# Up projections of the FFN: one 512-column matmul for high and low x in place of two of 256

## What is computed

```python
u = rms_norm_2(h, pre_ffn_norm[i])
up = causal_dwconv(u @ w_up[i], conv_w[i], conv_b[i])     # w_up: 2048 x 11264
gate, val = jnp.split(up, 2, axis=-1)
f = (jax.nn.gelu(gate, approximate=True) * val) @ w_down[i]   # w_down: 5632 x 2048
h = h + rms_norm_2(f, post_ffn_norm[i])
```

## Time and profile before

| | |
|---|---|
| median of 3 runs | 2880.22 us (2879.9 to 2881.02) |
| span of the profiled execution | 2875.0 us |
| instructions | 51385 |
| mean granted TensorE clock over the span | 0.943 of full speed |

### The profile page before, as it was taken

How to read it: one execution, slowest core, us unless ns; L and a number is a source line. 1 busy time by engine, 2 the same in 40 slices (tenths; PEclk the granted TensorE clock), 3 DMA queues, 4 the chain that set the end, 5 groups by cost and what they waited for, 6 DMA issues and landing times.

```text
span 2875.0 us, 51385 instructions
## 1 busy us (share of the span) xinstructions
PE 2619.4 (91%) x22498; PEld 2563.1 (89%) x22498; DVE 1685.9 (59%) x1516; ACT 1104.7 (38%) x1093; POOL 217.8 (8%) x117
## 2 busy tenths in 40 slices
PE   5999999979999787987998999998999999999986
PEld 5999999879999787886886999987999999999986
DVE  4556666475455785284363445557666666666665
ACT  3344545333333351242233333433344444444442
POOL 3000000023400231041000000002000000000000
PEclk9999999989999898798796999998999999999998
DMA  5444444334445342041140555552455555555432
GB/s 189 149 147 157 145 149 144 123 112 155 161 167 180 125 153 80 18 147 44 46 163 29 190 183 182 179 185 109 164 188 184 181 190 177 188 185 180 175 132 88
DMA packets 59615, 419.95 MB, mean 146 GB/s; under 512 B 6464, under 2 KB 8640, under 8 KB 9056
## 3 DMA queue, kind: packets, MB, share of 16 engines
q1 hardware_dynamic: 59280, 417.26, 40.8%
q0 software_dynamic: 208, 0.75, 0.1%
HBM read 415.89 MB, written 2.10 MB: 145 GB/s over the span
## 4 chain that ended last, share of the span: by engine, by line
PE 79%; DVE 13%; ACT 4%; issue 2%; POOL 2%; DMA 0%; SPq 0%; DVEq 0%; ACTq 0%; POOLq 0%
PE banks L206 23%; PE banks L208 23%; PE banks L207 23%; DVE weights_lo_sb L191 3%; ACT weights_hi_sb L185 2%; DVE xa_lo_sb L269 2%; DVE h_sb L259 1%; PE banks L1005 1%; PE banks L240 1%; PE banks L916 1%; PE banks L995 1%; PE banks L1004 1%; POOL rw_tile_sb L1156 1%; PE banks L1389 1%; PE banks L373 1%
## 5 line engine op out<-in xcount | busy, mean ns | idle before, releaser
L206 PE MATMUL banks<-xa_hi_sb,weights_hi_sb 128*128 128x256 f32 (+1 forms) x4800 | 1382.0, 288 | 106.0 <-DVE weights_lo_sb L191 47.2
L191 DVE TENSOR_TENSOR weights_lo_sb<-raw_weights_sb,weights_hi_sb 128x2048 fp32r<-128x2048 f32 x393 | 914.3, 2328 | 800.6 <-ACT weights_hi_sb L185 798.3
L207 PE MATMUL banks<-xa_lo_sb,weights_hi_sb 128*128 128x256 f32 (+1 forms) x4800 | 1376.9, 287 | 0.0
L208 PE MATMUL banks<-xa_hi_sb,weights_lo_sb 128*128 128x256 f32 (+1 forms) x4800 | 1376.7, 287 | 0.0
L185 ACT CAST weights_hi_sb<-raw_weights_sb 128x2048 fp32r<-128x2048 f32 x393 | 748.5, 1905 | 1107.8 <-PE banks L208 1095.4
L206 PEld LDWEIGHTS banks<-xa_hi_sb,weights_hi_sb 128*128 128x128 f32 x4800 | 923.2, 192 | 116.4 <-issue 50.5
L208 PEld LDWEIGHTS banks<-xa_hi_sb,weights_lo_sb 128*128 128x128 f32 x4800 | 923.1, 192 | 0.0
L207 PEld LDWEIGHTS banks<-xa_lo_sb,weights_hi_sb 128*128 128x128 f32 x4800 | 919.5, 192 | 0.5
L206 PE MATMUL banks<-ff_hi_sb,weights_hi_sb 128*128 128x256 f32 x704 | 198.4, 282 | 3.1 <-DVE ff_lo_sb L1887 2.7
L206 PE MATMUL banks<-xb_hi_sb,weights_hi_sb 128*128 128x256 f32 (+1 forms) x688 | 197.2, 287 | 4.0 <-DVE low_flat_sb L1514 1.3
L207 PE MATMUL banks<-ff_lo_sb,weights_hi_sb 128*128 128x256 f32 x704 | 199.7, 284 | 0.0
(11 more groups left out here) (365 smaller groups left out, 2148.0 us busy)
## 6 DMA issues: line engine op xcount, KB each, us to landing
raw_weights_sb<-weights SPq DMA_DIRECT2D x393, 1024.0 KB, 4.8
h_sb<-h SPq DMA_DIRECT2D x1, 2176.0 KB, 8.8
out<-h_sb SPq DMA_DIRECT2D x4, 512.0 KB, 2.8
masks_sb<-consts_rw POOLq DMA_DIRECT2D x1, 352.0 KB, 3.9
params_sb<-params SPq DMA_DIRECT2D x1, 305.5 KB, 8.2
consts_first_sb<-consts_first SPq DMA_DIRECT2D x1, 304.0 KB, 9.4
...
```

The lines of the kernel that those rows point to most:

```text
L191: dve.tensor_tensor(c.w_lo[n % SPLIT][:], c.raw[n % RAW][:], c.w_hi[n % SPLIT][:].bitcast(F32), ALU.subtract).then_inc(c.sem("lo_done"), 1)
L206: pe.matmul(out, w_hi[:, k, a], x_hi[:, tile, cols], start=begin, stop=False)
L207: pe.matmul(out, w_hi[:, k, a], x_lo[:, tile, cols], start=False, stop=False)
L208: done = pe.matmul(out, w_lo[:, k, a], x_hi[:, tile, cols], start=False, stop=end)
```

## The change

The high and low parts of x now lie in one tensor, `xa_both` (128 x 2 x 16 x 272), and `xa` is two views of it. The up projections use a new function, `products_both`. Its first matmul reads high and low x together as 512 columns and writes a whole bank, columns 0 to 255 with high weights by high x, 256 to 511 with high weights by low x. Its second adds low weights by high x. The two halves of a bank are summed when they are taken: ACT copies the upper columns of the four banks to `low_half` (the tile `late_acc`), DVE adds the lower columns (`up_summed`) and then multiplies by `rs`. PE waits for `up_summed` where it waited for `up_out_taken`. The down projections and all other stages keep `products`. Besides, several semaphores are merged into counted ones (`lam_steps`, `zeros`, `rw_taken`, `grams`, `grams_taken`, `ple_steps`), with the same waits; these edits are left out below.

```diff
-        self.xa = [self.sb(ctx, f"xa_{x}", [P, KT, ROWS], F32R) for x in ("hi", "lo")]
+        self.xa_both = self.sb(ctx, "xa", [P, 2, KT, ROWS], F32R)
+        self.xa = [self.xa_both[:, x] for x in range(2)]
...
+def products_both(c, pe, n, x, tiles, outs, cols, first, last, i=None, step=0, pause=None):
+
+    pe.wait_ge(c.sem("lo_done"), at(n + 1, i, step))
+    w_hi, w_lo = c.w_hi[n % SPLIT], c.w_lo[n % SPLIT]
+    length = cols.stop - cols.start
+    for j, out in outs:
+        if pause and j == 3:
+            pause()
+        for k, tile in tiles:
+            a = slice(j * P, j * P + P)
+            begin, end = first and k == tiles[0][0], last and k == tiles[-1][0]
+            pe.matmul(out, w_hi[:, k, a], x[:, :, tile, cols], start=begin, stop=False)
+            done = pe.matmul(out[:, length:], w_lo[:, k, a], x[:, 0, tile, cols], start=False, stop=end)
+    done.then_inc(c.sem("slot_used"), 1)
...
-    first_chunk_pe(c, pe, t, n, c.xa, 3, BOTH, 6, 4)
+    for s in range(4):
+        pe.wait_ge(S("x_ready"), 12 + s + 1)
+        products_both(c, pe, n + s, c.xa_both, t4(s), banks(c, 0, 2 * SEQ), BOTH, s == 0, s == 3)
+    sum_squares(c, pe, t["acc"], 7, BOTH, S("squares_ready"), 4, S("stats_done"))
...
-                pe.wait_ge(S("up_out_taken"), i * 2 + 1)
+                pe.wait_ge(S("up_summed"), i * 2 + 1)
...
-                products(c, pe, n + 8 + 4 * x + s, c.xa, t4(s), banks(c, x, SEQ), BOTH, s == 0, s == 3, i, 12)
+                products_both(c, pe, n + 8 + 4 * x + s, c.xa_both, t4(s), banks(c, x, 2 * SEQ), BOTH, s == 0, s == 3, i, 12)
...
+    def low(x, f, i, done):
+
+        act.wait_ge(S("slot_used"), done)
+        act.copy(t["low_half"][:], c.ps[:, 4 * x:4 * x + 4, SEQ:2 * SEQ]).then_inc(S("up_low"), 1)
...
+    low(0, 0, None, n + 4)
     scaled(0, 0, None)
     for m in range(6, 9):
         split_hi(c, act, n + m)
+    act.wait_ge(S("up_summed"), 1)
+    low(1, 0, None, n + 8)
     gelu(0, None)
     scaled(1, 0, None)
...
         for m in range(1, 13):
+            if m in (5, 9):
+                act.wait_ge(S("up_summed"), at(m // 4 + 1, i, 2))
+                low(m // 4 - 1, 1, i, at(n + 8 + m - 1, i, 12))
             split_hi(c, act, n + 8 + m, i, 12)
...
     def taken(x, f, i, done):
-        dve.wait_ge(S("slot_used"), done)
-        dve.tensor_tensor(t["up"][x][:, :, 2:], out(x), wide(t["rs"][:, BOTH], 4), ALU.mult).then_inc(S("up_out_taken"), 1)
+        up = t["up"][x][:, :, 2:]
+        dve.wait_ge(S("up_low"), at(2 * f + x + 1, i, 2))
+        dve.tensor_tensor(up, out(x), t["low_half"][:], ALU.add).then_inc(S("up_summed"), 1)
+        dve.wait_ge(S("up_summed"), at(2 * f + x + 1, i, 2))
+        dve.tensor_tensor(up, up, wide(t["rs"][:, BOTH], 4), ALU.mult).then_inc(S("up_out_taken"), 1)
...
+            m["low_half"] = late["acc"][:, :, 0:SEQ]
```

More of the change, by code:

```diff
@@ L366, in attn_pe @@
     ps, S = c.ps, c.sem
-    pe.wait_ge(S("lam_products"), 1)
-    pe.matmul(ps[:, 4, 0:2], c.const("ones"), t["lam"][:, 0:2], start=True, stop=True).then_inc(S("lam_sums"), 1)
+    pe.wait_ge(S("lam_steps"), 1)
+    pe.matmul(ps[:, 4, 0:2], c.const("ones"), t["lam"][:, 0:2], start=True, stop=True).then_inc(S("lam_steps"), 1)
     def scores(v):
@@ L466, in attn_act @@
     operands_act(c, act, 0, slice(0, ROWS), "pre0", 0)
-    act.wait_ge(S("lam_sums"), 1)
-    act.activation(t["lam"][:, 2:4], ps[:, 4, 0:2], ACT.Exp).then_inc(S("lam_exps"), 1)
+    act.wait_ge(S("lam_steps"), 2)
+    act.activation(t["lam"][:, 2:4], ps[:, 4, 0:2], ACT.Exp).then_inc(S("lam_steps"), 1)
     def head(h, i, proj, cur, old):
@@ L601, in head @@
             if h == 1:
-                dve.wait_ge(S("zeros_ready"), 1)
+                dve.wait_ge(S("zeros"), 1)
             for q, a, b, keys in BLOCKS:
@@ L965, in rw_pe @@
         pe.wait_ge(S("bonus_taken"), b + 1)
-        for base, src, done in ((0, t["bt"], "gram_b"), (4, t["kt"], "gram_k")):
+        for base, src in ((0, t["bt"]), (4, t["kt"])):
             if base:
-                pe.wait_ge(S("rw_v_taken"), b + 1)
+                pe.wait_ge(S("rw_taken"), 3 * b + 3)
             for j in range(4):
@@ L974, in rw_pe @@
                                       src[at_[p], j, cuts[x]], t["ar"][at_[p], j, x, :], start=True, stop=True)
-            m.then_inc(S(done), 1)
-        pe.wait_ge(S("gram_b_taken"), b + 1)
+            m.then_inc(S("grams"), 1)
+        pe.wait_ge(S("grams_taken"), 3 * b + 1)
         for j in range(4):
@@ L982, in rw_pe @@
                                   t["ar"][at_[p], j, x, 0:64], t["bt"][at_[p], j, cuts[x]], start=True, stop=True)
-        m.then_inc(S("gram_l"), 1)
-        pe.wait_ge(S("gram_k_taken"), b + 1)
-        pe.wait_ge(S("gram_l_taken"), b + 1)
+        m.then_inc(S("grams"), 1)
+        pe.wait_ge(S("grams_taken"), 3 * b + 3)
         for level in range(1, 6):
@@ L1153, in rw_pool @@
             rw_gated(c, t, pool, st, 0)
-        pool.wait_ge(S("rw_k_taken_out"), b + 1)
+        pool.wait_ge(S("rw_taken_out"), 3 * b + 1)
         for j in range(4):
@@ L1269, in rw_dve @@
         st.did(dve.tensor_tensor(t["xx"][:], t["ll"][:], mask("level0"), ALU.mult))
-        dve.tensor_tensor(t["xx"][:], t["xx"][:], mask("eye"), ALU.add).then_inc(S("gram_l_taken"), 1)
-        dve.wait_ge(S("gram_l_taken"), b + 1)
+        dve.tensor_tensor(t["xx"][:], t["xx"][:], mask("eye"), ALU.add).then_inc(S("grams_taken"), 1)
+        dve.wait_ge(S("grams_taken"), 3 * b + 3)
         for level in range(1, 6):
@@ L1691, in ffn_pe @@
     t4 = lambda s: [(k, 4 * s + k) for k in range(4)]
-    first_chunk_pe(c, pe, t, n, c.xa, 3, BOTH, 6, 4)
+    for s in range(4):
+        pe.wait_ge(S("x_ready"), 12 + s + 1)
+        products_both(c, pe, n + s, c.xa_both, t4(s), banks(c, 0, 2 * SEQ), BOTH, s == 0, s == 3)
+    sum_squares(c, pe, t["acc"], 7, BOTH, S("squares_ready"), 4, S("stats_done"))
     for s in range(4):
         pause = (lambda: pe.wait_ge(S("root_done"), 7)) if s == 0 else None
-        products(c, pe, n + 4 + s, c.xa, t4(s), banks(c, 1, SEQ), BOTH, s == 0, s == 3, pause=pause)
+        products_both(c, pe, n + 4 + s, c.xa_both, t4(s), banks(c, 1, 2 * SEQ), BOTH, s == 0, s == 3, pause=pause)
     def down(n, x, i=None):
@@ L1714, in ffn_pe @@
             if x < 2:
-                pe.wait_ge(S("up_out_taken"), i * 2 + (3 + x))
+                pe.wait_ge(S("up_summed"), i * 2 + (3 + x))
             else:
@@ L1739, in ple @@
         m.then_inc(S("slot_used" if j2 else "ple_done"), 1)
-    pe.wait_ge(S("ple_ready"), 1)
+    pe.wait_ge(S("ple_steps"), 2)
     pe.wait_ge(S("y_taken"), 15)
@@ L1796, in ffn_act @@
     act.wait_ge(S("ple_in"), 16)
-    act.copy(t["ple_hi"][:], t["ple"][:]).then_inc(S("ple_hi"), 1)
+    act.copy(t["ple_hi"][:], t["ple"][:]).then_inc(S("ple_steps"), 1)
     with act.Fori(0, FF_STEPS - 1) as i:
         for m in range(1, 13):
+            if m in (5, 9):
+                act.wait_ge(S("up_summed"), at(m // 4 + 1, i, 2))
+                low(m // 4 - 1, 1, i, at(n + 8 + m - 1, i, 12))
             split_hi(c, act, n + 8 + m, i, 12)
@@ L1892, in ffn_dve @@
     pre_root_dve(c, dve, st, t, 6, BOTH)
-    dve.wait_ge(S("ffn_zeros"), 1)
+    dve.wait_ge(S("zeros"), 3)
     taken(0, 0, None, n + 4)
```

46 lines of the change are left out of this document (23 added, 23 removed).

## The result

The changed kernel takes **2884.59 us** (median of 20 runs, 2878.9 to 2890.25), the kernel before on the same chip 2879.89 us (20 runs, 2875.81 to 2882.41). The ratio is **1.0014, with a 95% interval from 1.0008 to 1.0021**: slower by 0.14%, or 4.0 us (2.3 to 6.0). That is less than the 0.2% that the prediction took as the bound of no change, but the interval leaves no doubt of its sign, and it is not the forecast one. 2875.5 us was forecast; 2884.6 is inside the range and 0.7 us from rival (a), whose 2885.3 us stand for "the cost goes by columns".

What follows compares the result with a forecast made beforehand. TensorE was taken as the bound (91% busy, 79% of the chain of waits). Saving 14.8 us, waits +6.9 and start +3.2 give -4.7 us on the 2875.0 span; with 5.2 up to the median, 2875.5 us, range 2864 to 2890.

Steps and rivals of the forecast that it cites:

- the bound of no change: Whole kernel: a measurement tells 0.2%, 5.8 us, from no change; the forecast of 0.16% down lies near that bound.
- rival (a): Up-projection matmuls: cost goes by columns, 512 take 233.9 ns, only 3.5 us saved, slower at 2885.3 us; chance 0.30.
- The saving: Up projections in the FFN loop: 11.6 ns fixed per matmul, saved in each of 1280 triples, 14.8 us.
- 229 ns: Time of the 512-column matmul at which savings and costs are equal, about 7.6 ns saved a triple.
- The waits: FFN loop, TensorE after each take: 0.48 us at gate half, 0.21 at value half, 6.9 us over 10 turns.
- The chain of 5.78 us: Gate-half take in the loop: copy, add, multiplication, low split, then matmul take 5.78 us; TensorE wants the slot at 5.30.
- (c): Loop takes: waits longer than 0.69 us a step because delay passes to the next slot; 2885.5 us, chance 0.10.
- (d): Up projections: the 512-column matmul is issued as two, so rival (a) without saving; chance 0.02.
- The start: Start of the FFN: the two takes ahead of the loop delay TensorE, 3.2 us lost.
- The bound given for the clock: TensorE's restart at the FFN start: costed at nothing more, at most another 2 us of half speed, 1 us lost.
- The rule of the Trainium skill: Matmuls in a row: N/2.4 + 2.5 ns each, so merging saves only 2.5 ns a triple, 3.2 us.

## Why the prediction was wrong

The account had the right terms (fewer matmuls, two waits a turn, a later start), but its largest term was mis-sized, because the split of a matmul's time into a fixed part and one by columns was wrong. The sign hung on that term: with 5.7 ns saved and the prediction's own waits and start the sum is +1.8 us (-7.3 + 5.9 + 3.2); with 11.6 ns saved, the measured start and the measured waits (0.9 us longer in all behind the shorter slots) it is still -1.5.

- **The saving: this step failed.** "I take them as fixed per matmul with its load": 11.6 ns a triple. Measured are 5.7, and 0.44 ns a column in place of 0.417. The two neighbours had been read: 16 columns between 256 and 272 cost 7.9 ns, which spoke for columns, and the plain float32 matmul at 216, which showed no such surplus. The text called the 7.9 ns nearer to a cost by columns, and still chose the fixed price, on the strength of rows of another number format and of the half clock. The 7.9 ns were the only row of the same format at the same clock. The inference that the surplus comes only at full clock held; that it is the same at 512 columns did not: 17.6 ns, not 11.6. 14.8 us became 7.3.
- **Rival (a) was near by luck in part.** It says that the 512-column matmul decides at 229 ns. It took 230.9, and the kernel is slower. But 229 rests on the prediction's waits and start; with those measured (12.4 us together) the balance would lie at some 226 ns, an estimate from these sums. And (a)'s 2885.3 us, 0.7 from the measured time, come of errors that cancel: it saves 3.5 us where 7.3 were saved, and loses 8.6 where 12.4 were lost. Its direction was right, its 233.9 ns were 3.0 too many.
- **The waits.** The chain of 5.78 us held to the hundredth. With the slot as it came out (5.59) it gives 0.38 and 0.21; what was missing is the 0.11 us that the first matmul after a wait takes on top, at each of two takes: 0.38 + 0.21 + 0.22 = 0.81, measured 0.83. 8.3 us instead of 6.9. Nothing passed on to the next slot, so (c) fell in the form given. (d) fell with the rows of 128x512.
- **The start.** 3.2 us forecast, 3.6 of later restart and 0.5 of longer half clock. At the first take the wait grew from 0.49 to 1.89, 1.40 instead of 1.27, and the slots up to the next wait gave back 0.23 in place of 2 x 0.19. The bound given for the clock (1 us) held it.
- **Sum.** -7.3 + 8.3 + 4.1 = +5.1 us by the same account (+5.5 with the loop read from its turns), -4.7 forecast; 7.5 of the difference is the first term, 1.4 the second, 0.9 the third.
- **The rule of the Trainium skill** ("TensorE: Matmul & The Clock Gate", section on the back-to-back issue gap), columns / 2.4 + 2.5 ns, which that section calls the gap of an isolated matmul, gives 109 and 216. The trace has 118.3 and 230.9 and disagrees with both. Its saving of 2.5 ns a triple is 3.2 under the measured 5.7, the forecast's 11.6 is 5.9 over it: as a warning against the merge the rule was the better guide, as a price it was not one.
